# Latent attention: the Scalar engine's copy of an item's transposed probabilities, placed ahead of the exponential of two items later

## The reference, cut to what matters

```python
def _attend(q, k, v):
    s = jnp.einsum('bqhd,bkhd->bhqk', q * q.shape[-1] ** -0.5, k).astype(jnp.float32)
    p = jax.nn.softmax(s, axis=-1).astype(v.dtype)
    return jnp.einsum('bhqk,bkhd->bqhd', p, v)

def _blocked_attention(q, k, v):
    B, S, H, dq = q.shape
    qb = q.reshape(B, S // ATTN_QBLOCK, ATTN_QBLOCK, H, dq).swapaxes(0, 1)
    out = lax.map(lambda qq: _attend(qq, k, v), qb)
    return out.swapaxes(0, 1).reshape(B, S, H, v.shape[-1])
...
o_mla = _blocked_attention(q_mla, k_mla, v_mla)
y = _merge(o_na, o_mla, ga, gb, w_o_na[l], w_o_mla[l], w_out[l])
```

## Time and profile before

| what | value |
|---|---|
| median of 3 executions | 2457.29 us (2456.32 to 2460.51) |
| the profiled execution, its own time | 2457.69 us |
| its span | 2455.9 us |
| PE busy | 2326.6 us, 95% of the span |
| ACT busy | 873.8 us, 36% |
| DVE busy | 895.8 us, 36% |
| POOL busy | 1107.1 us, 45% |
| mean granted clock of PE | 0.985 of full speed |
| share of the chain that ended last | PE 57%, POOL 20%, issue 20%, DVE 2%, ACT 1% |

### The profile page before, as it was taken

How to read it: one execution, slowest core, us unless ns; L and a number is a source line. 1 busy time by engine, 2 the same in 40 slices (tenths; PEclk the granted TensorE clock), 3 DMA queues, 4 the chain that set the end, 5 groups by cost and what they waited for, 6 DMA issues and landing times.

```text
span 2455.9 us, 33124 instructions
## 1 busy us (share of the span) xinstructions
PE 2326.6 (95%) x11964; PEld 1880.9 (77%) x11964; DVE 895.8 (36%) x1525; ACT 873.8 (36%) x1239; POOL 1107.1 (45%) x1356
## 2 busy tenths in 40 slices
PE   6999899889999999999999999999998898999997
PEld 5778687667788878888888878877765585888885
DVE  3325532476778671111111144243035544111113
ACT  3454443434233443212211233255334534423222
POOL 3343364166888764333333343332440054555554
PEclk9999999999999999999999999999999998999998
DMA  4222132245555532211211221222220021232222
GB/s 157 87 77 78 59 122 78 104 147 178 197 187 198 183 109 69 69 60 61 69 61 60 69 69 67 78 86 78 80 90 18 1 89 54 98 100 97 95 95 94
DMA packets 66603, 231.35 MB, mean 94 GB/s; under 512 B 7216, under 2 KB 9520, under 8 KB 66352
## 3 DMA queue, kind: packets, MB, share of 16 engines
q1 hardware_dynamic: 50656, 180.02, 21.7%
q10 hardware_dynamic: 15824, 49.55, 5.9%
HBM read 226.66 MB, written 2.10 MB: 93 GB/s over the span
## 4 chain that ended last, share of the span: by engine, by line
PE 57%; POOL 20%; issue 20%; DVE 2%; ACT 1%; POOLq 0%; DMA 0%; ACTq 0%; DVEq 0%; SPq 0%
PE ps L1744 36%; POOL WLO L335 20%; PE ps L1762 9%; PE ps L2252 4%; PE ps L1777 1%; PE ps L2374 1%; PE ps L2223 1%; PE ps L2237 1%; PE ps L2194 1%; PE ps L2363 1%; ACT MPT L897 1%; DVE stat L1613 1%; PE ps L2209 0%; PE ps L2403 0%; PE ps L2336 0%
## 5 line engine op out<-in xcount | busy, mean ns | idle before, releaser
L335 POOL TENSOR_TENSOR WLO<-RAW,WHI 128x256 fp32r<-128x256 f32 x1340 | 1091.5, 848 | 1300.4 <-ACT WHI L370 1299.8
L370 ACT ACTIVATE WHI<-RAW 128x1024 fp32r<-128x1024 f32 x335 | 354.3, 1059 | 697.1 <-DMA RAW<-in_stream_dram 673.6
L1744 PE MATMUL ps<-HLO,WHI 128*128 128x512 f32 (+2 forms) x1368 | 456.4, 367 | 10.3 <-DVE XK L1249 2.4
L1744 PE MATMUL ps<-HHI,WHI 128*128 128x512 f32 (+2 forms) x1368 | 448.9, 361 | 0.0
L1744 PE MATMUL ps<-HHI,WLO 128*128 128x512 f32 (+2 forms) x1368 | 448.6, 361 | 0.0
L1744 PEld LDWEIGHTS ps<-HLO,WHI 128*128 128x128 f32 (+1 forms) x1368 | 237.4, 188 | 58.2 <-issue 4.0
L1744 PEld LDWEIGHTS ps<-HHI,WHI 128*128 128x128 f32 (+1 forms) x1368 | 237.6, 188 | 43.3 <-issue 3.3
L1744 PEld LDWEIGHTS ps<-HHI,WLO 128*128 128x128 f32 (+1 forms) x1368 | 237.8, 188 | 41.1
L1342 DVE TENSOR_TENSOR SF<-SF,ps 128x512 f32<-128x512 f32 (+1 forms) x66 | 51.2, 776 | 542.5 <-PE ps L1744 379.7
L1744 PE MATMUL ps<-GLO,WHI 128*128 128x512 f32 (+1 forms) x704 | 232.0, 365 | 5.3 <-DVE GLO L1347 2.9
L1744 PE MATMUL ps<-GHI,WLO 128*128 128x512 f32 (+1 forms) x704 | 231.5, 364 | 0.0
(11 more groups left out here) (365 smaller groups left out, 3032.0 us busy)
## 6 DMA issues: line engine op xcount, KB each, us to landing
RAW<-in_stream_dram SPq DMA_DIRECT2D x335, 512.0 KB, 3.3
ADA<-in_ada_dram ACTq DMA_DIRECT2D x72, 512.0 KB, 4.0
BM<-in_bias_dram ACTq DMA_DIRECT2D x8, 448.0 KB, 3.7
DECAY<-in_decay_dram ACTq DMA_DIRECT2D x4, 512.0 KB, 4.4
out_dram<-X SPq DMA_DIRECT2D x8, 256.0 KB, 2.1
X<-in_x_dram SPq DMA_DIRECT2D x2, 512.0 KB, 5.6
X<-in_x_dram ACTq DMA_DIRECT2D x2, 512.0 KB, 6.7
C<-in_mem_dram ACTq DMA_DIRECT2D x1, 1024.0 KB, 5.5
```

Source lines behind the costliest of these rows:

```text
L335: op = nc.gpsimd.tensor_tensor(WLO[:, slot(u), k:k + 2], RAW[:, slot(u), k:k + 2], WHI[:, slot(u), k:k + 2].bitcast(F32), ALU.subtract)
L370: nc.scalar.activation(WHI[:, j], RAW[:, j], ACT.Copy).then_inc(unit_hi, 1)
L1744: mm = nc.tensor.matmul(out, w, x[:, k, tok], start=(k == 0 and n == 0), stop=(k == kt - 1 and n == 2))
```

## The change

In ACT's turn the two steps change places: the copy of item n-2 comes first, the exponential of item n second. The waits and the instructions are the same, and so are the other engines' programs.

```diff
             def attend(scale):
 
                 for n in range(MLA_ITEMS + 5):
+                    k = n - 2
+                    if 0 <= k < MLA_ITEMS:
+                        act.wait_ge(*attend_at("t", k + 1))
+                        if k >= 4:
+                            act.wait_ge(*attend_at("o", k // 2 - 1))
+                        nc.scalar.activation(MPT[:, k % 4], psf[:, 2048:2048 + N2], ACT.Copy).then_inc(s("attend_at"), 1)
                     if n < MLA_ITEMS:
                         act.wait_ge(*attend_at("m", n + 1))
                         if n >= 3:
...
                         nc.scalar.activation(MP[:, n % 3], psf[:, at:at + N2], ACT.Exp, scale=scale,
                                              bias=stat[:, n % 3, 1:2], accum_out=stat[:, n % 3, 2:3]).then_inc(s("attend_e"), 1)
-                    k = n - 2
-                    if 0 <= k < MLA_ITEMS:
-                        act.wait_ge(*attend_at("t", k + 1))
-                        if k >= 4:
-                            act.wait_ge(*attend_at("o", k // 2 - 1))
-                        nc.scalar.activation(MPT[:, k % 4], psf[:, 2048:2048 + N2], ACT.Copy).then_inc(s("attend_at"), 1)
                     k = n - 4
```

## The result

| kernel | median us | range | executions |
|---|---|---|---|
| before | 2457.35 | 2456.32 to 2460.51 | 4 |
| with the change | 2441.33 | 2439.38 to 2444.10 | 4 |

The ratio is 0.9935 (95% interval 0.9924 to 0.9947): 16.0 us less. The forecast was 2440.9.

What follows compares the result with a forecast made beforehand. A loop of waits, not an engine, was taken to bound the latent attention: 15.0 - 0.6 + 1.36 + 1.29 - 0.7 = 16.4 us less, for a median of 2440.9 us. The forecast's own range was 2438.6 to 2444.5.

Steps and rivals of the forecast that it cites:

- The loop of waits: Latent attention: no engine is full; a pair takes 6.60 us because C(5) waits behind E(7), starting 1.36 us late.
- gains nothing: Even item's copy ahead of its exponential: no gain, and E(6) starts 2.87 us later, just in time for S(8).
- PE's loop: PE's own sum for a pair after the change: 4.13 + 1.40 = 5.53 us, bounds 5.42 and 5.64.
- ACT's loop: Second closed loop, through the even item's copy and exponential: E to S to V to T to C to E, 5.53 us.
- 0.70 to 0.75 from T to S: Sign of a right forecast in the profile after: an interval of this many us from T to S on PE.
- small slips, 0.05 a pair: Two loops of the same length drive one another, so slips don't average out: 0.7 us taken off the gain.
- 0.6 for the head pairs: Three times the third step (MOHI, MOLO) delays the next maximum and weighing: 0.2 us each, bounds 0 and 0.69.
- The clock's return at V(14): With PE idle 1.1 us instead of 2.31 ahead of V(14), V(14) runs at full speed: 1.29 us gained.
- The gain ahead of V(0): V(0) too was counted as coming one interval earlier, as one of the 14 gains of 6.60 - 5.53 us.
- rival 1: The exponential E comes too late: C to E 1.06, a pair 5.89 to 6.1 us, total 2445 to 2449; chance 0.14.
- Nothing comes out of it: What PE gains it loses later, waiting for weights or other engines: 2457 us, within 5 us; chance 0.05.
- The clock falls: The new pattern holds PE at 1.2 GHz, 10.74 us a pair, up to 58 us more, 2515; chance 0.03.

Runs made afterwards that it cites:

- the 0.41 us put there: The changed kernel with one more, unused ACT copy between C(n-2) and E(n) of every even n: 6.018 us a pair, median 2447.54 us, ratio 0.9958 to before.
- the mixed version: Against the kernel before, odd items' copies go first, and of the even ones only those of turns 12, 20 and 28: median 2441.35 us, ratio 0.9929.

## Why the prediction was right

**What bounds the stage.** The loop of waits was read rightly from the one pair: take C(odd) out from behind E(odd) and it opens. Moving the odd copies alone gives the plain pairs even a little more than the change; moving the even ones alone gives nothing. One step was wrong in a part: "gains nothing" for the even item's copy holds for the ten plain intervals only. The odd copies alone gave 10.46 of the 12.81 us between V(0) and V(13); the other 2.35 are what the even copies save at the three head pairs, less 0.1 in each plain pair.

**PE's loop.** Forecast 5.53, with 1.40 for S to V, which no row showed. The variant with the odd copies alone has it pure: 5.51, with 1.39.

**ACT's loop.** Forecast 5.53 as well, measured 5.606. Its links were C to E 0.70 (0.70 measured), E to S 1.05 (1.05), V to T 1.47 (1.46) and T to C 0.91 (0.91). The missing 0.08 is in S to V, 1.48 and not 1.40: S(8) starts on time, 0.66 behind T(5) as before, and loses 0.09 over its matmuls when it was released by E at the last moment. So the sign "0.70 to 0.75 from T to S" did not show at this junction. The step "small slips, 0.05 a pair" stood for this and came out at 0.08. The "slack used up to the last hundredth" was right, as the 0.41 us put there shows, which came back as 0.412. That ACT works strictly in the order of its program does cost something here, 0.1 us a pair, and not the 2.87 that E's delay would be by itself. By the rule of the Trainium skill (TensorE: Matmul & The Clock Gate, on the array's architectural detail) E(even) can't pass C; the traces agree: E(6) starts 0.70 behind C(4) in the changed kernel, and in no trace does an E start ahead of the copy in front of it.

**The terms of the sum.** Between V(0) and V(13) I had 13 of the 14 gains of 1.07, less 0.6 for the head pairs and 0.65 of the slips: 12.7. Measured: 12.81. The loss at the head pairs did not come (5.61 there, too): in the changed order the delay of `MOLO` runs in time that the even copy's wait leaves free. The 0.6 for it, within its bounds of 0 and 0.69 each, was mis-sized; it made up for slips that were larger than 0.05. V(13) to V(14): forecast 1.36, measured 1.41. The clock's return at V(14): forecast 1.29, measured 1.30 of the 1.40 by which V(14) to V(15) shrank. The gain ahead of V(0), forecast 1.07, is the term that single traces can't show. From E(0) to V(0) before has 10.22, and the changed kernel's three traces have 9.51, 9.58 and 8.11; the variant that moves C(29) alone, with the same order as before up to there, has 9.20. PE runs there at its lower clock after 2.7 to 3.3 us of standing still, and when the full clock comes back differs from one execution to the next. The first pair of traces gives 0.71.

**What of it was luck.** The stage shrank by 16.3 us in the first pair of traces, and the sum was 16.4. That it is so close is partly luck: the head pairs cost nothing in place of 0.6 and the end gave 0.16 more than forecast, while the slips took some 0.3 more between V(0) and V(13) than allowed and the start gave less than 1.07 in this pair of traces. The measured 16.0 has itself an interval of 13.0 to 18.7 us. Two of the bounds were added up loosely: 5.42 a pair without slips gives 18.6 and not 18.7, and rival 1 with 6.1 a pair is 8.0 us short of the forecast and not 7 (its 2449 fits the 8.0).

**The rivals.** *E too late*: the 0.26 between copy and exponential was no price of changing over; it is gone in the changed kernel, with 0.70 from start to start. *Nothing comes out of it*: the rest of the program took 488 us behind V(15) both times, and 486.9 to 488.1 in all eleven traces. *The clock falls*: it stood at 1.00 from 1866 to 1958. Each was tested in the place that the forecast named.

## What to carry to other kernels

Before two steps of an in-order engine are swapped, write down for each of the two who waits for it next and how long that one is still busy: the odd copy's consumer stood idle, the even exponential's consumer came 2.87 us later, and that told the gain and its limit. When a loop opens, sum the other loops link by link as well; the next one may be within 0.1 us of it, and an instruction of known length put into it tells its slack one for one. A reordering that fits the plain turns must be followed through the turns with something extra in them: here three of thirteen intervals took back 3.6 us of a variant that looked better in the other ten.

## What the runs showed of the hardware that was not expected

- A busy PE is not a fast PE: from 1866 to 1942 us the changed kernel shows 76.00 of 76.00 us busy, with 5.606 us a pair, and the mixed version has no gap either (70.00 of 70.00 us from 1866 to 1936), with 5.51 in its plain pairs. The 0.09 us that S(n+2) loses behind E do not show as idle time; only with the 0.41 us added does the profile name the wait (0.24 us).
- After PE had stood still for 3.3 us at the start of the stage, E(0) to V(0) took 9.58 us in one trace of the changed kernel and 8.11 in another, by how soon the granted clock went from 1.2 back to 2.4 GHz. Read in steps of half a microsecond, it stood at 0.50 from 1862.5 to 1868.5 us in the first, and from 1863.0 to 1866.0 in the second. At the end of the stage, behind 2.31 us of idle time, its mean was 0.68 from 1958 to 1963 in the trace of before. With 1.01 us of idle time, once per pair, it never fell: 1.00 from 1866 to 1958.
- The way from the program's start to the stage, the same in all kernels, took 1850.67 us in one trace and 1856.52 in another. Differences of an us or two between kernels have to be read inside the stage.
